# Forget decay of eight attention heads: a table per head, built by GpSimd from key sums, in place of decay matmuls

## The reference, cut to what matters

```python
log_f = jax.nn.log_sigmoid(ff.astype(f32) + fox_forget_bias.astype(f32))
cum_f = jnp.transpose(jnp.cumsum(log_f, axis=1), (0, 2, 1))
...
s = jnp.einsum("bqhd,bkhd->bhqk", qf_b, kf).astype(f32) * scale
s = s + cq[..., None] - cum_f[:, :, None, :]
p = _masked_softmax(s, key_pos[None, :] <= tpos[:, None])
o_fox = jnp.einsum("bhqk,bkhd->bqhd", p.astype(dt), vf)
```

## Time and profile before

| | us |
|---|---|
| runs of the kernel | 2304.01, 2306.86, 2308.09 (median 2306.86) |
| the profiled execution | 2309.19 |
| its span in the trace | 2307.1 |
| mean granted clock of TensorE | 0.992 |
| chunk 10 of the input stage | 244 to 269 |
| FOX scores, first to last | 263 to 302 |
| end of the first attention's jobs | about 350 |

### The profile page before, as it was taken

One profiled execution on the slowest core, in us unless ns is written; L12 is line 12 of the kernel. 1 busy time (PEld: TensorE's weight loads), 2 busy tenths in 40 slices (PEclk: granted clock), 3 DMA queues, 4 the chain that ended last, 5 costly groups with the idle time before them and its releaser, 6 DMA issues.

```text
span 2307.1 us, 29343 instructions
## 1 busy us (share of the span) xinstructions
PE 2262.2 (98%) x10352; PEld 1868.1 (81%) x10352; DVE 1514.5 (66%) x1952; ACT 1086.2 (47%) x1515; POOL 173.2 (8%) x193
## 2 busy tenths in 40 slices
PE   9999999999999999999989999989999999999998
PEld 7888877888888888888868887777888888888886
DVE  6555377767777777777766886776777544554555
ACT  6555464544444444344345776654443344444444
POOL 4000100000000000000001885000000000000000
PEclk9999999999999999999989999999999999999999
DMA  7566517688888888888766664676887666666664
GB/s 232 178 182 189 160 47 288 223 266 280 277 281 286 277 276 280 282 279 277 266 200 191 192 183 127 214 260 188 283 277 264 190 190 188 191 191 192 191 189 147
DMA packets 274503, 511.79 MB, mean 222 GB/s; under 512 B 20071, under 2 KB 28949, under 8 KB 274124
## 3 DMA queue, kind: packets, MB, share of 16 engines
q1 hardware_dynamic: 270252, 509.94, 69.6%
q10 hardware_dynamic: 4128, 0.26, 0.1%
HBM read 508.04 MB, written 2.10 MB: 221 GB/s over the span
## 4 chain that ended last, share of the span: by engine, by line
PE 93%; DVE 3%; issue 2%; DMA 1%; ACT 1%; SPq 0%; DVEq 0%; ACTq 0%
PE bank L945 30%; PE bank L961 28%; PE bank L962 28%; PE bank L916 1%; PE bank L1018 1%; DMA raw<-in_w_out 1%; PE bank L1091 1%; PE bank L930 1%; DVE ada_acc L1784 1%; PE bank L1006 1%; DVE w_lo L1807 1%; ACT w_hi L1388 0%; PE bank L1059 0%; PE bank L1047 0%; PE bank L818 0%
## 5 line engine op out<-in xcount | busy, mean ns | idle before, releaser
L1807 DVE TENSOR_TENSOR w_lo<-raw,w_hi 128x1024 fp32r<-128x1024 f32 x760 | 936.9, 1236 | 593.8 <-ACT w_hi L1388 585.0
L1388 ACT ACTIVATE w_hi<-raw 128x1024 fp32r<-128x1024 f32 x760 | 802.4, 1059 | 978.8 <-PE bank L945 912.2
L961 PE MATMUL bank<-w_hi,act_hi 128*128 128x512 f32 x2016 | 792.2, 393 | 0.0
L962 PE MATMUL bank<-w_hi,act_lo 128*128 128x512 f32 x2016 | 786.0, 390 | 0.0
L945 PE MATMUL bank<-w_lo,act_hi 128*128 128x512 f32 x2080 | 558.9, 391 | 0.0
L945 PEld LDWEIGHTS bank<-w_lo,act_hi 128*128 128x128 f32 x2080 | 392.1, 189 | 82.6
L962 PEld LDWEIGHTS bank<-w_hi,act_lo 128*128 128x128 f32 x2016 | 379.2, 188 | 77.9 <-issue 0.7
L961 PEld LDWEIGHTS bank<-w_hi,act_hi 128*128 128x128 f32 x2016 | 379.1, 188 | 77.8 <-issue 0.7
L961 PE MATMUL bank<-w_hi,mid_hi 128*128 128x512 f32 x960 | 379.5, 395 | 6.8 <-ACT w_hi L1388 5.6
L962 PE MATMUL bank<-w_hi,mid_lo 128*128 128x512 f32 x960 | 374.7, 390 | 0.0
L1784 DVE SCALAR_TENSOR_TENSOR ada_acc<-ada_raw,c_act,ada_acc 128x512 f32<-128x512 f32 x360 | 269.7, 749 | 9.0 <-DMA ada_raw<-in_ada_w 1.9
(11 more groups left out here) (272 smaller groups left out, 1007.1 us busy)
## 6 DMA issues: line engine op xcount, KB each, us to landing
ada_raw<-in_ada_w SPq DMA_DIRECT2D x192, 512.0 KB, 5.2
raw<-in_w_gate SPq DMA_DIRECT2D x176, 512.0 KB, 4.4
raw<-in_w_up SPq DMA_DIRECT2D x176, 512.0 KB, 4.4
raw<-in_w_down SPq DMA_DIRECT2D x176, 512.0 KB, 4.3
raw<-in_w_in SPq DMA_DIRECT2D x168, 512.0 KB, 3.8
raw<-in_w_out SPq DMA_DIRECT2D x64, 512.0 KB, 5.5
raw<-in_cmp_w_k SPq DMA_DIRECT2D x4, 512.0 KB, 4.5
raw<-in_cmp_w_v SPq DMA_DIRECT2D x4, 512.0 KB, 4.7
```

Of the source, the lines that this page charges most:

```text
L961: pe.matmul(A_[t][:, :], h_, w_hi[:, s, kk, :], start=(k == 0), stop=False)
L962: pe.matmul(A_[t][:, :], l_, w_hi[:, s, kk, :], start=False, stop=False)
L1388: act.activation(w_hi[:, U % SPLIT_SLOTS].rearrange("p k n -> p (k n)"), raw[:, R % RAW_SLOTS].rearrange("p k n -> p (k n)"), ACT.Copy).th ...
L1807: dve.tensor_tensor(w_lo[:, U % SPLIT_SLOTS].rearrange("p k n -> p (k n)"), raw[:, R % RAW_SLOTS].rearrange("p k n -> p (k n)"), w_hi[:, U ...
```

## The change

GpSimd's `after_key` and spans and TensorE's decay matmuls go. In their place:

- GpSimd zeroes `spread` (it lies where `ws` was, so it waits for `small_mm`). VectorE copies the logs of the eight heads into it, each at the first of 32 columns, in chunk 7 after unit 1 (`spread_made`).
- TensorE multiplies `spread` with the triangle and with ones after unit 6 of chunk 7 (`cum_gemm`, six matmuls of 128 columns). The result has one head's running sums over the 256 keys in each of the rows 0, 32, 64 and 96, for two groups of four heads.
- VectorE copies it into `cumT` in chunk 8 after unit 1 (`cum_copied`).
- GpSimd then makes a table of 384 columns for each head: a broadcast of the head's row to all partitions, and two subtractions from the mask, chained by semaphores (`decay_made`). Five tables lie in `tabs`, over buffers of the beginning; those of heads 5 and 6 lie in `ysb`, that of head 7 in `zsb`, so head 5 waits for `turned`.
- VectorE's reduction waits for `decay_made` and adds the head's table in place of the mask.
- The first piece of the compression on TensorE waits for `cum_copied`, since both use `MISC[0]`.

```diff
+        decays = ExitStack()
+        N_TABS = 5
+        tabs = sb("tabs", [P, N_TABS, TAB], F32, decays)
+        decays.close()
...
+        A1 = ExitStack()
+        spread = sb("spread", [P, TT, 2, 4, 32], F32, A1)
+        cumT = sb("cumT", [P, 2, T], F32, A1)
+        A1.close()
...
-        def span_of(j):
-
-            return ysb[:, j % 2, 0:T].rearrange("p (t q) -> p t q", q=P)
+        def decay_of(h):
+
+            if h < N_TABS:
+                return tabs[:, h, :]
+            two = ysb[:, :, :].rearrange("p a b -> p (a b)")
+            return two[:, (h - N_TABS) * TAB:(h - N_TABS + 1) * TAB] if h < N_TABS + 2 else zsb[:, 0, 0:TAB]
...
-            link(pool.memset(after_key[:, :], 1.0))
-            link(pool.affine_select(out=after_key[:, P:T], in_=after_key[:, P:T], pattern=[[-1, P]],
-                                    compare_op=ALU.is_ge, fill=0.0, base=-1, channel_multiplier=1))
...
-            pool.wait_ge(lf_d, 2)
-            pool.wait_ge(turned, len([c for _, c in IN1 if c[0] != "value"]))
-            for j in range(FOX_H):
-                if j >= 2:
-                    pool.wait_ge(scored, j - 1)
-                pool.tensor_scalar(span_of(j)[:, 0, :], upper[:, :], lf[:, 5, 0, j:j + 1], None, ALU.mult)
-                pool.tensor_scalar(span_of(j)[:, 1, :], upper[:, :], lf[:, 5, 1, j:j + 1], None,
-                                   ALU.mult).then_inc(span_ready, 1)
+            pool.wait_ge(small_mm, 1)
+            pool.memset(spread[:, :, :, :, :], 0.0).then_inc(spread_zero, 1)
+            pool.wait_ge(cum_copied, 1)
+            pool.wait_ge(cols_turned, 1)
+            pool.wait_ge(ws_split, 1)
+            for h in range(FOX_H):
+                if h == N_TABS:
+                    pool.wait_ge(turned, len([c for _, c in IN1 if c[0] != "value"]))
+                tab, r0 = decay_of(h), 32 * (h % 4)
+                if h >= 1:
+                    pool.wait_ge(decay_made, h)
+                link(pool.partition_broadcast(tab[:, P:TAB], cumT[r0:r0 + 1, h // 4, :]))
+                link(pool.tensor_tensor(tab[:, 0:P], mask[:, P:T], tab[:, P:2 * P], ALU.subtract))
+                pool.tensor_tensor(tab[:, P:TAB], mask[:, :], tab[:, P:TAB], ALU.subtract).then_inc(decay_made, 1)
...
+                elif c is S_IN1[SMALL_OUT + 2]:
+                    gemm(c, r, after=lambda u: cum_gemm() if u == 6 else None)
...
+            def cum_gemm():
+
+                pe.wait_ge(spread_made, 1)
+                pe.wait_ge(small_out, 1)
+                for g in range(2):
+                    st = [spread[:, t, g, :, :].rearrange("p a m -> p (a m)") for t in range(TT)]
+                    o = MISC[0][:, g * T:(g + 1) * T]
+                    pe.matmul(o[:, 0:P], st[0], upper[:, :], start=True, stop=True)
+                    pe.matmul(o[:, P:T], st[0], ones[:, :], start=True, stop=False)
+                    ins = pe.matmul(o[:, P:T], st[1], upper[:, :], start=False, stop=True)
+                ins.then_inc(cum_summed, 1)
...
-                                    start=True, stop=not b["decay"])
-                    if b["decay"]:
-                        h = b["h"]
-                        pe.wait_ge(span_ready, j + 1)
-                        if t == 1:
-                            pe.matmul(s[:, c0:c0 + P], lf[:, 5, 0, h:h + 1].to_broadcast([P, P]),
-                                      after_key[:, P:T], start=False, stop=False)
-                        ins = pe.matmul(s[:, c0:c0 + n], span_of(j)[:, t, :], after_key[:, T - n:T], start=False,
-                                        stop=True)
+                                    start=True, stop=True)
...
                 pe.wait_ge(blk_zero, kind + 1)
+                pe.wait_ge(cum_copied, 1)
                 pe.wait_ge(blk_ready, 4 * (kind + 1))
...
+                    if c is S_IN1[SMALL_OUT + 3] and u == 1:
+                        dve.wait_ge(cum_summed, 1)
+                        dve.tensor_copy(cumT[:, :, :].rearrange("p g t -> p (g t)"), MISC[0][:, :]).then_inc(
+                            cum_copied, 1)
                     if c is S_IN1[SMALL_OUT + 2] and u == 1:
                         dve.wait_ge(lf_a, 1)
                         dve.tensor_tensor(lf[:, 5], lf[:, 3], lf[:, 4], ALU.subtract).then_inc(lf_d, 1)
+                        dve.wait_ge(lf_d, 2)
+                        dve.wait_ge(spread_zero, 1)
+                        dve.tensor_copy(spread[:, :, :, :, 0], lf[:, 5].rearrange("p t (g a) -> p t g a", a=4)).then_inc(
+                            spread_made, 1)
...
+                        if b["decay"]:
+                            dve.wait_ge(decay_made, b["h"] + 1)
                         dve.wait_ge(scored, i + 1)
...
                             dve.tensor_tensor_reduce(cost_of(i)[:, c0:c0 + n], bank[2 + i % 2][:, c0:c0 + n],
-                                                     tab[:, T - n:T], 1.0, 3.0e38, ALU.add, ALU.min,
+                                                     decay_of(b["h"])[:, c0:c0 + n] if b["decay"] else tab[:, T - n:T],
+                                                     1.0, 3.0e38, ALU.add, ALU.min,
```

More of the change, by code:

```diff
@@ L411, in build_two_blocks @@
         upper = sb("upper", [P, P], F32, A)
-        after_key = sb("after_key", [P, T], F32, A)
         mask = sb("mask", [P, T], F32, A)
@@ L497, in build_two_blocks @@
             sem("vc_ready"), sem("pick_made"))
-        lf_a, lf_d, span_ready = sem("lf_a"), sem("lf_d"), sem("span_ready")
+        lf_a, lf_d, spread_zero, spread_made = sem("lf_a"), sem("lf_d"), sem("spread_zero"), sem("spread_made")
+        cum_summed, cum_copied, decay_made = sem("cum_summed"), sem("cum_copied"), sem("decay_made")
         gate_exp, gates_ready = sem("gate_exp"), sem("gates_ready")
@@ L1862, in attend @@
                         b = JOBS[i]
-                        tab = {"mask": lambda: mask[:, :], "mask2": lambda: mask2[:, :],
-                               "alibi": lambda: alibi[:, b["h"], :]}[b["table"]]()
+                        tab = {"mask2": lambda: mask2[:, :], "alibi": lambda: alibi[:, b["h"], :],
+                               "mask": lambda: None}[b["table"]]()
+                        if b["decay"]:
+                            dve.wait_ge(decay_made, b["h"] + 1)
                         dve.wait_ge(scored, i + 1)
```

## The result

| | before, us | after, us |
|---|---|---|
| median, first measurement | 2305.82 (4 runs, 2304.01 to 2308.09) | 2324.57 (4 runs, 2320.54 to 2326.80) |
| median, second measurement | 2308.18 (16 runs, 2303.97 to 2310.38) | 2322.55 (6 runs, 2315.78 to 2325.00) |
| profiled execution; its span | 2309.19; 2307.1 | 2320.54; 2318.8 |
| mean granted clock of TensorE | 0.992 | 0.988 |

The changed kernel is slower: ratio 1.0079, 95% interval 1.0061 to 1.0096, in the first measurement, and 1.0059 (1.0047 to 1.0071) in the second. That is under 1%, but both intervals lie clear of 1. The forecast was 2329.5 us, with a stated range from 2300 to 2347 us; its case "code swaps" alone ran from 2312 to 2347 us.

The account below looks back on a forecast made before the run. TensorE was taken to bound the kernel until 302.6 us, then VectorE; head 7's table 19.8 us late plus 2.9 us of slow clock gave +22.7 us, 2329.5 us against the median of 2306.86, range 2300 to 2347 us.

Parts of the forecast that it names:

- code swaps: GpSimd loading code between broadcasts and subtractions in every head, L above 13.3 us: 2312 to 2347 us, chance 0.69.
- Removed and added on TensorE: 24 decay matmuls gone, 7.0 us; six sum matmuls added in chunk 7, 1.3 us; net -5.6 us on TensorE.
- VectorE's copies: Small spread copy 0.17 us, sums copy in chunk 8 0.69 us, done at 198.4 us; split 0.8 us late, costing nothing.
- When the tables are wanted: VectorE's reductions want the tables of heads 5 to 7 at 290.0, 293.4, 296.9 us; covered up to L = 12.3 us.
- The turn L: GpSimd's time per head's table: two code swaps of 6.5 us plus 2.5 us work, 15.5 us; head 7 19.8 us later.
- After the stall: From head 7's reduction the delay goes through whole; TensorE's slow clock adds 2.9 us, bounded by 0 and 6 us.
- The sum: Whole kernel: +19.8 us late reduction plus 2.9 us clock, +22.7 us; TensorE's net -5.6 us already included.
- Covered: Rival: no swap or L up to 12.4 us, so TensorE's net -5.6 us arrives: 2301.3 us, chance 0.21.
- The broadcast is slow: Rival: GpSimd's broadcast itself slow, or loads waiting behind weight traffic; L = 19 us, kernel 2360 us, chance 0.04.
- Shared access: Rival: GpSimd's subtractions slow VectorE's splits through shared access to memory; judged to cost nothing, no chance of its own.

Follow-up runs that it names:

- selects: Changed kernel with each head's two GpSimd subtractions replaced by two affine selects, VectorE negating the sums: 2300.37 us, ratio 0.9973; run again without an edit, 2301.33 us, ratio 0.9974.
- the repeat: The changed kernel run again without an edit: 2322.55 us (6 runs), ratio 1.0059 to the kernel before.
- two groups: Changed kernel with GpSimd's broadcasts of heads 0 to 4 together, then their subtractions, and likewise heads 5 to 7: 2301.59 us, ratio 0.9976 to before.
- no tables: Changed kernel without GpSimd's table loop, plain mask in the reductions, so forget decay is left out of the scores: 2301.42 us, ratio 0.9973 to before.

## Why the prediction was right, step by step

**Removed and added on TensorE: right.** Net -5.6 us was forecast. The three kernels in which tables are early or absent (one of them run twice) show -5.5 to -5.6 us in the trace and -5.9 to -7.2 us in the medians. The six matmuls of the sums, in TensorE's timeline of the changed kernel, first and last, with what follows:

```profile
195.54 0.38 PE L917 MATMUL bank<-upper,spread 128*128 128x128 f32 x2
...
196.65 0.39 PE L919 MATMUL bank<-upper,spread 128*128 128x128 f32 x2
196.79 0.48 PE L989 MATMUL bank<-w_hi,act_hi 128*128 128x512 f32 x1
```

From 195.54 to 196.79 us they take 1.25 us; 1.3 was forecast.

**VectorE's copies: right.** The copy of the sums took 0.69 us, as forecast from the row of its size:

```profile
197.07 0.69 DVE L1865 COPY cumT<-bank 128x512 f32<-128x512 f32 x1 [1.68 <-PE bank L919]
197.68 1.22 DVE L1828 TENSOR_TENSOR w_lo<-raw,w_hi 128x1024 fp32r<-128x1024 f32 x1
```

The sums were there 0.64 us before the forecast 198.4 us, and the split behind the copy held nobody up: TensorE was busy 23.00 of the 23.00 us from 189 to 212 us.

**When the tables are wanted: right as far as tested.** Forecast: 290.0, 293.4 and 296.9 us for heads 5 to 7. With selects (second run) the reductions stood at 289.86, 293.29 and 296.82 us, 0.25 us of idle time ahead of the last where 0.15 was left by the forecast. So the 296.9 us from which the break at a turn of 12.3 us was worked out is confirmed; no run had a turn near 12.3 us.

**The turn L: right in where the price stands and how often, near in size partly by luck.** 15.5 us was forecast, 15.0 us measured; tables forecast for 291.4, 306.9 and 322.4 us let the reductions start at 289.36, 303.39 and 318.27 us. The forecast had head 5's reduction wait too: in this execution its table was there at 288.38 us, 1 us before the reduction, and in the repeat the reduction waited 1.04 us. Of the 4.3 us by which the last table was early, 0.5 are the earlier start (197.91 us and not 198.4), 3.0 the work (2.1 us a head, not 2.5: the broadcast of 0.55 us was met, the subtractions took 0.45 and 0.73 us and not 0.60 and 1.00), and 0.7 the gaps: sixteen of 6.5 us were forecast, 104 us, and fifteen with a mean of 6.9 us came, 103.3 us. The sixteenth, ahead of the first broadcast, would lie in GpSimd's wait of 90 us for the sums, if it is there at all. It was an error of the forecast to count it, and by luck it was cancelled by gaps that were longer.

The size came from landings of transfers of 5.5 and 7.5 us. That the middle of the two came out is luck too, and no proof of the reason given there. The gaps hardly follow the queues: in the changed kernel those ahead of subtractions are 7.1 to 8.5 us where the DMA share is 0.54 to 0.82, 7.43 us (head 4) where it is 0.01, and 6.90 to 7.18 us (heads 7 and 6) where no packet moves. What the engine does in a gap was not shown; "code" is a name for it here, and that it is fetched stays open. The Trainium skill (GPSIMD Engine Reference, Instruction dispatch) has about 6 us for the first call of a newly loaded routine, with no instruction in the profile; that a load stands in these gaps is not shown. The trace agrees with 6 us ahead of broadcasts (5.8 to 6.1 us in six of seven cases) and is 1.5 us above it ahead of subtractions; by that rule's number the last table was to come at 313.6 us, as far below the measured 318.1 as the forecast was above.

**After the stall: half right.** The delay went through whole, as said. The granted clock fell, as said. These are windows of the changed kernel (stretch, width, busy time of TensorE, its weight loads, VectorE, ScalarE, GpSimd, then clock, DMA share, GB/s), to be held against the earlier trace rows:

```profile
300.00:305.00 5.00, 0.24 (x1) 0.24 (x2) 1.57 (x9) 1.27 (x6) 1.17 (x2) 0.50 0.00 0
305.00:310.00 5.00, 3.22 (x11) 2.32 (x10) 0.63 (x2) 0.35 (x2) 0.55 (x1) 0.67 0.00 0
310.00:315.00 5.00, 0.00 (x0) 0.00 (x0) 0.00 (x0) 0.00 (x0) 0.00 (x1) 0.68 0.00 0
315.00:320.00 5.00, 0.36 (x2) 0.36 (x3) 1.69 (x9) 1.39 (x6) 1.17 (x2) 0.50 0.00 0
320.00:325.00 5.00, 5.00 (x19) 4.32 (x18) 4.83 (x18) 2.92 (x11) 0.00 (x0) 0.50 0.00 0
325.00:330.00 5.00, 4.58 (x28) 3.55 (x27) 4.72 (x24) 3.33 (x13) 0.00 (x0) 0.96 0.01 2
```

TensorE was busy for 3.8 of the 20 us from 300 to 320 us. Its clock had fallen to 0.50 (1.2 GHz) already in 300 to 305 us, earlier than the forecast 305; it stood between the two levels on average from 305 to 315 us and at 0.50 again until about 325 us. But the 2.9 us priced for it were the term that was mis-sized: they measured 0. (The two pieces of the chain that the forecast pointed at differ by 5.46 - 2.76 = 2.7 us, so the term was 0.2 us off its own source as well.) From head 7's reduction to the transpose at the end of VectorE's stretch it is 10.48 us before and 10.48 us after:

```profile
328.75 0.55 PE bank L1067 x3
```

This is the row of the chain of waits after, and 328.75 - 318.27 = 10.48; in the chain of before the same step runs from 302.58 us to 313.06 us. In 320 to 325 us TensorE is busy all of the time at half speed, and VectorE is the bound nevertheless: it is busy 4.83 of 5 us, and the chain of waits stays on it from 318.57 to 328.75 us. Nor does the clock cost anything later, by the times from head 7's reduction to the end given under the table. The forecast named that bound (0, since VectorE sets the pace) and took the middle.

**The sum.** +22.7 us forecast; +16.4 and +17.1 us in the two traces, +18.8 and +14.4 us by the medians. The forecast was too high in each, and inside its range. What is missing in the first trace: the last table 4.3 us early, the clock 2.9 us, and the forecast was made against before's own start, 0.7 us later than this one's: 22.7 - 4.3 - 2.9 + 0.7 = 16.2.

**The profiled pair** differs by only 11.4 us (11.7 in the spans), the medians by 18.8. Against the +16.4 us at head 7 the spans lack 4.7 us: 0.7 are the start, and 3.0 lie far behind the change, in sixteen matmuls `conv_sq` that run at either clock level in one and the same kernel (0.9 us stay open). Their line in the changed kernel and in its repeat: duration in ns, least, median, most, then first and last start:

```profile
L1177 PE MATMUL bank<-conv_sq,ones x16: 379/379/483, 1454.2 to 1457.5; 128*128 128x256 f32 x16
```

```profile
L1177 PE MATMUL bank<-conv_sq,ones x16: 379/634/794, 1455.3 to 1461.6; 128*128 128x256 f32 x16
```

From first to last start 3.3 us in the one execution, at a clock of 1.00, and 6.3 us in the other, at 0.55; the profile of before had 6.4 us, at a median of 634 ns and a clock of 0.54. The spans of the two profiles of the changed kernel (2318.8 and 2321.9 us) and those of the two with selects (2296.8 and 2299.6 us) differ by these 3 us. A pair of single executions can't be read to better than that.

**The rivals.** "Covered" did not come about here, but its number was right: 2301.3 us forecast, 2300.4 and 2301.3 us measured once the gaps are avoided. "The broadcast is slow" falls with 0.55 us (1.40 us the first time). "Shared access" of subtractions falls with "two groups": all its subtractions run, and it stands at 123.69 us in the table and -5.9 us by the medians, against 123.59 us and -6.8 us with no tables.

## What to carry to other kernels

On GpSimd the order of the kinds of operation can be a cost of its own. Shown here are three kinds: broadcast and subtraction do not go together, a select goes with either; no other pair was run in alternation. Before work is moved there, list the kinds in program order, look for a gap that ends with "issue" wherever two kinds meet, and group by kind, or replace one kind by another that pays no gap; two selects in place of two subtractions turned +19 us into -7 us here, and kernel "selects" is faster than both kernels compared. A producer with slack is best checked as one number: the turn at which it becomes late (12.3 us here), against a turn that counts the gaps and not only the busy time (2.1 of 15.0 us). And TensorE's slow clock cost nothing here where VectorE set the pace (0 in place of 2.9 us): ask who is last at that place before a price is added.

## What the runs showed that was not expected

- Between broadcast and subtraction there is a gap at every change of kind, even for a subtraction of 0.19 us; selects run beside either at no price (at most 0.17 us from one to the next).
- The two directions differ: 6.8 to 9.0 us ahead of a subtraction, 5.7 to 7.9 us ahead of a broadcast, over all kernels here. How much the transfers have to do with it is open: with the queues idle or nearly so the first is 6.8 to 7.4 us in the changed kernel and its repeat.
- The gap ahead of head 5's broadcast is longer than the others of its direction in every kernel that alternates in each head: 6.84 to 7.91 us in five profiles, against 5.73 to 6.57 us. Head 5 has one more semaphore wait in the program, long met by then, and its table is the first in another buffer. Whether either costs the 1 to 1.5 us is open; no run tested it.
- A change of kind that falls into a long wait is free: in "two groups" the broadcasts at 260 us follow TensorE's turn within 0.1 us of the kernel with selects. The first broadcast, too, starts 0.15 us after the sums are copied; whether it had anything to change is not shown.
